# Two blocks in fp32 on one core: the moving operands of FFN matmuls read in two halves by turns

## The reference

```python
def swiglu(h, w_gate, w_up, w_down):
    return (jax.nn.silu(h @ w_gate) * (h @ w_up)) @ w_down
# h: 256 x 1024, w_gate and w_up: 1024 x 2816, w_down: 2816 x 1024
# first stack, twice per layer:  x = x + 0.5 * swiglu(rmsnorm(x, g), w_gate, w_up, w_down)
# second stack, once per layer:
gu = x @ w_gate_up[l]
hidden = jax.nn.silu(gu[..., :D_FF_2]) * gu[..., D_FF_2:]
x = _layer_norm(DEEPNORM_ALPHA * x + hidden @ w_down[l], ln2_g[l], ln2_b[l])
```

## Time and profile before

| | us |
|---|---|
| median of 2 runs | 2010.06 (2009.33 to 2010.79) |
| span of the profiled execution | 2008.8 |
| PE busy in the span | 1995.9 (99%) |
| PE weight loads busy | 1934.1 (96%) |
| DVE busy | 1238.7 (62%) |
| ACT busy | 997.1 (50%) |
| DMA engines, mean busy share of the slices | about one half |

### The profile page before, as it was taken

How to read it: one execution, slowest core, us unless ns; L and a number is a source line. 1 busy time by engine, 2 the same in 40 slices (tenths; PEclk the granted TensorE clock), 3 DMA queues, 4 the chain that set the end, 5 groups by cost and what they waited for, 6 DMA issues and landing times.

```text
span 2008.8 us, 37237 instructions
## 1 busy us (share of the span) xinstructions
PE 1995.9 (99%) x15798; PEld 1934.1 (96%) x15798; DVE 1238.7 (62%) x1214; ACT 997.1 (50%) x997; POOL 55.2 (3%) x49
## 2 busy tenths in 40 slices
PE   9999999999999999999999999999999999999998
PEld 8999999999999999899999999999998999999997
DVE  7556665755675576766556664585447574576445
ACT  6545655544454457654444575444444573644442
POOL 3000000100010000010000000000000000000000
PEclk9999999999999999999999999999999999999999
DMA  8555453455555554345554453555554544564552
GB/s 306 189 188 188 169 171 145 167 189 188 188 195 187 186 186 147 126 153 213 188 188 169 179 189 128 213 206 189 188 186 158 191 167 149 210 224 162 187 187 100
DMA packets 52913, 363.29 MB, mean 181 GB/s; under 512 B 5960, under 2 KB 7120, under 8 KB 9808
## 3 DMA queue, kind: packets, MB, share of 16 engines
q1 hardware_dynamic: 51200, 352.99, 48.9%
q0 software_dynamic: 1616, 8.86, 1.2%
HBM read 360.76 MB, written 1.06 MB: 180 GB/s over the span
## 4 chain that ended last, share of the span: by engine, by line
PE 95%; DVE 3%; ACT 1%; DMA 1%; issue 0%; DVEq 0%; SPq 0%; ACTq 0%
PE ps L277 21%; PE ps L279 21%; PE ps L278 21%; PE ps L322 4%; PE ps L323 4%; PE ps L324 4%; PE ps L560 3%; PE ps L561 3%; PE ps L559 3%; PE ps L543 1%; PE ps L537 1%; PE ps L538 1%; PE ps L1864 1%; PE ps L843 1%; DMA raw<-in_slots 1%; PE ps L311 1%
## 5 line engine op out<-in xcount | busy, mean ns | idle before, releaser
L247 DVE TENSOR_TENSOR wlo<-raw,whi 128x2048 fp32r<-128x2048 f32 x322 | 742.9, 2309 | 421.0 <-ACT whi L242 420.2
L277 PE MATMUL ps<-in_hi,whi 128*128 128x256 f32 x3236 | 909.6, 281 | 1.1 <-DVE in_lo L652 0.9
L278 PE MATMUL ps<-in_lo,whi 128*128 128x256 f32 x3236 | 903.4, 279 | 0.0
L279 PE MATMUL ps<-in_hi,wlo 128*128 128x256 f32 x3236 | 902.4, 279 | 0.0
L242 ACT ACTIVATE whi<-raw 128x2048 fp32r<-128x2048 f32 x322 | 614.5, 1910 | 196.6 <-PE ps L279 173.8
L277 PEld LDWEIGHTS ps<-in_hi,whi 128*128 128x128 f32 x3236 | 608.2, 188 | 4.8 <-DVE wlo L263 1.4
L278 PEld LDWEIGHTS ps<-in_lo,whi 128*128 128x128 f32 x3236 | 608.3, 188 | 2.3 <-issue 0.7
L279 PEld LDWEIGHTS ps<-in_hi,wlo 128*128 128x128 f32 x3236 | 608.3, 188 | 0.0
L322 PE MATMUL ps<-whi,in_hi 128*128 128x256 f32 x640 | 181.4, 283 | 0.0
L323 PE MATMUL ps<-wlo,in_hi 128*128 128x256 f32 x640 | 179.8, 281 | 0.0
L324 PE MATMUL ps<-whi,in_lo 128*128 128x256 f32 x640 | 179.8, 281 | 0.0
(11 more groups left out here) (318 smaller groups left out, 2188.2 us busy)
## 6 DMA issues: line engine op xcount, KB each, us to landing
raw<-in_slots SPq DMA_DIRECT2D x330, 1024.0 KB, 4.8
ws<-in_lngb POOLq DMA_DIRECT2D x4, 1024.0 KB, 6.0
raw<-in_slots SPq DMA_DIRECT2D x12, 256.0 KB, 5.6
ws<-in_mem_t POOLq DMA_DIRECT2D x2, 1024.0 KB, 10.2
consts<-in_consts SPq DMA_DIRECT2D x1, 1536.0 KB, 9.6
consts<-in_consts POOLq DMA_DIRECT2D x1, 1472.0 KB, 8.1
x<-in_x_t SPq DMA_DIRECT2D x4, 256.0 KB, 5.1
ws<-m_rows POOLq DMA_DIRECT2D x2, 512.0 KB, 5.5
```

The costliest lines, as they stand in the source:

```text
L247: dve.tensor_tensor(wlo[:, j], raw[:, j], whi[:, j].bitcast(F32), ALU.subtract).then_inc(lo_ready, 1)
L277: pe.matmul(out, whi[:, j, o:o + n], hi, start=start, stop=False, skip_group_check=True)
L278: pe.matmul(out, whi[:, j, o:o + n], lo, start=False, stop=False, skip_group_check=True)
L279: return pe.matmul(out, wlo[:, j, o:o + n], hi, start=False, stop=stop, skip_group_check=True)
```

## The change

The change touches only the access patterns of some matmuls. The new helper `halves_by_turns(v, run)` takes a view of n columns, cuts it into two halves of n/2 columns, and walks them by turns: `run` columns of the first half, `run` columns of the second, the next `run` of the first, and so on. It is applied to the moving operand and to the output alike, so each product lands where it did, and only the order in which the columns pass through PE is another. For 256 columns the two halves are 512 bytes apart in SBUF and in PSUM, for 512 columns 1024 bytes. With `run` None the view stays as it was. The stationary operands, the number of instructions, their order on every engine, the waits and the DMAs stay as they were.

```diff
+        def halves_by_turns(v, run):
+
+            return v if run is None else v.rearrange("p (s a b) -> p a s b", s=2, b=run)
+
-        def pe_pair(pe, out, j, at=range(DT)):
+        def pe_pair(pe, out, j, at=range(DT), run=None):
 
             for m in range(2):
                 for k in range(DT):
-                    last = pe_weight(pe, out[:, m * T:(m + 1) * T], j, k * 256 + m * P, in_hi[:, at[k]], in_lo[:, at[k]],
+                    last = pe_weight(pe, halves_by_turns(out[:, m * T:(m + 1) * T], run), j, k * 256 + m * P,
+                                     halves_by_turns(in_hi[:, at[k]], run), halves_by_turns(in_lo[:, at[k]], run),
                                      k == 0, k == DT - 1)
             return last
+
+        GATE_RUN = (None, 4, 8, 2, 64, None)
+        DOWN_RUN = (None, None, None, 8, 4, 2)
...
-                pe_pair(pe, out, (c + s) % RING).then_inc(slot_used, 1)
+                pe_pair(pe, out, (c + s) % RING, run=GATE_RUN[f]).then_inc(slot_used, 1)
...
-        def pe_down_part(pe, j, hi, lo, t, h, first=False):
+        def pe_down_part(pe, j, hi, lo, t, h, run, first=False):
 
-            o, a = ps[:, 2 * t + h, :], slice(t * P, (t + 1) * P)
+            o, a = halves_by_turns(ps[:, 2 * t + h, :], run), slice(t * P, (t + 1) * P)
             for kk in range(2):
                 w = slice(kk * D + h * 512, kk * D + h * 512 + 512)
-                pe.matmul(o, hi[:, kk, a], whi[:, j, w], start=(first and kk == 0), stop=False, skip_group_check=True)
-                pe.matmul(o, hi[:, kk, a], wlo[:, j, w], start=False, stop=False, skip_group_check=True)
-                last = pe.matmul(o, lo[:, kk, a], whi[:, j, w], start=False, stop=False, skip_group_check=True)
+                pe.matmul(o, hi[:, kk, a], halves_by_turns(whi[:, j, w], run), start=(first and kk == 0), stop=False, skip_group_check=True)
+                pe.matmul(o, hi[:, kk, a], halves_by_turns(wlo[:, j, w], run), start=False, stop=False, skip_group_check=True)
+                last = pe.matmul(o, lo[:, kk, a], halves_by_turns(whi[:, j, w], run), start=False, stop=False, skip_group_check=True)
             return last
```

More of the change, by code:

```diff
@@ L570, in gate @@
                 pe.wait_ge(ffn_silu, fb + i)
-                pe_pair(pe, gate_ps, (c + s) % RING).then_inc(slot_used, 1)
+                pe_pair(pe, gate_ps, (c + s) % RING, run=GATE_RUN[f]).then_inc(slot_used, 1)
             def up(i, s, i3):
@@ L575, in up @@
                 pe.wait_ge(ffn_mul, fb + i)
-                pe_pair(pe, up_ps, (c + s) % RING).then_inc(slot_used, 1)
+                pe_pair(pe, up_ps, (c + s) % RING, run=GATE_RUN[f]).then_inc(slot_used, 1)
             def down(i, s, i3, first=False):
@@ L582, in down @@
                     for h in range(2):
-                        last = pe_down_part(pe, (c + s) % RING, h_hi, h_lo, t, h, first)
+                        last = pe_down_part(pe, (c + s) % RING, h_hi, h_lo, t, h, DOWN_RUN[f], first)
                 last.then_inc(slot_used, 1)
@@ L621, in pe_ffn_tok @@
             for h in range(2):
-                pe_down_part(pe, s9 % RING, h_hi, h_lo, 0, h)
+                pe_down_part(pe, s9 % RING, h_hi, h_lo, 0, h, DOWN_RUN[f])
             pe.wait_ge(lo_ready, s10 + 1)
@@ L625, in pe_ffn_tok @@
             for h in range(2):
-                pe_down_part(pe, s10 % RING, last_hi, last_lo, 0, h).then_inc(down_half, 1)
+                pe_down_part(pe, s10 % RING, last_hi, last_lo, 0, h, DOWN_RUN[f]).then_inc(down_half, 1)
             for h in range(2):
-                last = pe_down_part(pe, s9 % RING, h_hi, h_lo, 1, h)
+                last = pe_down_part(pe, s9 % RING, h_hi, h_lo, 1, h, DOWN_RUN[f])
             last.then_inc(slot_used, 1)
-            pe_down_part(pe, s10 % RING, last_hi, last_lo, 1, 0).then_inc(down_half, 1)
+            pe_down_part(pe, s10 % RING, last_hi, last_lo, 1, 0, DOWN_RUN[f]).then_inc(down_half, 1)
             if m_out is not None:
                 pe_turn_y(pe, m_out, 0)
-            pe_down_part(pe, s10 % RING, last_hi, last_lo, 1, 1).then_inc(slot_used, 1)
+            pe_down_part(pe, s10 % RING, last_hi, last_lo, 1, 1, DOWN_RUN[f]).then_inc(slot_used, 1)
         def wait_down(dve, f, t, h):
```

## The result

The changed kernel takes 2109.15 us (median of 2 runs, 2108.17 to 2110.14) against 2010.06 us: ratio 1.049, 95% interval 1.0473 to 1.0507. It is slower by 5%; I had forecast no change; the time lies inside the range of 1990 to 2165 us, which was as wide as it was for a rival's sake (runs of 2 at half pace).

What follows compares the result with a forecast made beforehand. PE's own stream was taken to bound the kernel. The terms, 3840 x 0 + 792 x 0 = 0, left the 2008.8 us span, whose runs' median lies 1.3 us higher: 2010 us, range 1990 to 2165 for 8 in 10.

Steps and rivals of the forecast that it cites:

- What bounds the kernel: Whole kernel: PE's own stream is the time, busy 1995.9 of 2008.8 us, so each nanosecond on a matmul counts.
- Counts: Matmuls the change touches: 3840 gate and up of 256 columns in four FFNs, 792 down of 512 columns.
- No other engine hides or adds anything: FFN 4 round of 16.80 us: DVE busy 8.26, ACT 6.76, DMA 53%; PE could be 8% faster without running into them.
- The price per column: Changed gate, up and down matmuls, 634 us: pace stays 0.456 ns per column, 0 us added; chance of this forecast 0.60.
- The stall that I had measured myself: Plain fp32r stream: as if standing still 1.25 ns after every 32 columns, 116.7 ns for 256 where the clock allows 106.7.
- Half pace for runs of 2: Gate and up of FFN 3, down of FFN 5: plain fp32's pace, 95 + 52 us, 2158 us in all; chance 0.18.
- the case that I held likeliest: Whole kernel: no change in pace, or a few ns in one run; 2010 us, own range 1998 to 2040.
- A price per jump: All changed matmuls: every jump costs the 1.25 ns stall, dearer for shorter runs; 372 us more, 2382 us; chance 0.14.
- The stall goes away: Changed matmuls: alternating two places gives a bank time, removing the stall; 1962 us in full; chance 0.08, full or part.
- The bound of 48 us: Changed matmuls: the most the order could save by removing the stall, 25 + 9 + 14 us.
- The ratio of 256 to 512 columns: FFN 3 slots: 116.7 and 233.3 ns, exactly as their columns, so nothing is a cost per instruction or weight load.
- The rules of the Trainium skill: Changed matmuls: line rule gives 2010 us, non-contiguous rule slows all 634 us; issue-gap rule estimates 109.2 and 215.8 ns.

## Why the prediction was right and wrong

- *What bounds the kernel*: right. PE's stream is the time, and each ns of a matmul appeared in full; the table of slots gives the span's growth without a rest.
- *Counts*: 3840 and 792 matmuls, right. *No other engine hides or adds anything*: right.
- *The price per column, "I take 0"*: this step failed. I argued that the pace cares neither for the length nor for the place of the operand, and took it for a pace of the datapath that needs only two neighbours side by side. Plain streams of two lengths can't show that: both use whole lines one behind the other. In place of 0 the runs showed 8.9, 6.6, 49.9 and 0.5 ns per gate or up matmul for runs of 4, 8, 2 and 64, and 9.2, 20 and about 101 ns per down matmul for runs of 8, 4 and 2. The price is in reading the moving operand (2109.95 us with it alone turned, 2014.33 with the output alone), and it hangs on two things: whether a run fills aligned lines of 16 bytes (126.7 against 171 ns for runs of 4 moved by 8 bytes), and the step between the runs (113.4 to 139.0 ns for the same whole lines). How the reader works behind this stays open. The stall that I had measured myself was a sign that the stream had little to spare.
- *Half pace for runs of 2*: the right mechanism (more bytes come than the run uses, and they are thrown away), and the right place, between 2 and 4. The size was off: 95 and 52 us were forecast, 48 and 27 measured, since from two halves such runs take 166.6 ns; the 216 were borrowed from plain fp32, which has another reason to be slow. That runs of 2 take 226.6 ns from four parts, near the 216, is no merit of the working. And it is luck that the time lies in the range: the range came from this rival at twice its size, not from the case that I held likeliest (1998 to 2040).
- *A price per jump*: the order 64, 8, 4, 2 came out as this rival had it (117.2, 123.3, 126.7, 166.6 ns), but at 0.2 ns and not 1.25 ns a jump, and the shift by 8 bytes made the same jumps dear.
- *The stall goes away*: partly true, at a step that the change does not use. The bound of 48 us for the changed matmuls was too high: at 114.9 and 226.7 ns they would save an estimated 13 us (2880 x 1.8, 960 x 2.9 and 792 x 6.6 ns), and the 34 us found come from nearly all fp32r matmuls of the kernel. The ratio of 256 to 512 columns had told me that nothing is a cost per instruction or weight load; the floor of 111.4 ns was hidden, since it lies just under the 116.7 ns of the plain order.
- *The rules of the Trainium skill*: "Advanced Engine Details and Errata", section Memory Cachelines, asks for two hits on a 16-byte line. The runs agree with a line of that size, but two hits are not enough for fp32r: 166.6 to 233 ns against 116.7. Its other half, that a non-contiguous pattern slows matmuls, is said there of PSUM, and is not borne out here: the output turned alone left every slot at its pace. The estimate of 216 ns by "TensorE: Matmul & The Clock Gate", section Back-to-back issue gap, of the Trainium skill holds for bf16 with 512 columns (216 measured) and not for fp32r (233.3).

## What to carry to other kernels

Ask first whether each run of a moving operand fills whole, aligned lines of 16 bytes. In fp32r, runs that did cost from 3 ns less to 22 ns more per 256 columns, and runs that used half a line 50 to 116 ns more. A bf16 stream has more to spare: its runs of 8 bytes cost 5%, its runs of 4 bytes 26%. Then measure the step between the runs, since no count of lines or jumps here gives the price. And when a stream is slower than the clock allows, try the order of its columns: an order at no cost in instructions gave 1.7% here.

## What the runs showed of the hardware that I had not expected

- Reading in runs of 16 bytes at a step of 64 bytes is faster than reading in the order of addresses: 226.7 against 233.3 ns for 512 columns, 114.9 against 116.7 for 256. At a step of 256 bytes the same whole lines take 139.0 ns per 256 columns.
- fp32r instructions with 128 moving columns take 111.4 ns each, nearly what 256 columns do (116.7). The weight load of 128 columns is the likely floor; it was not measured apart.
- The output order was free: with the outputs alone in runs of 2, 4, 8 and 64 from two halves, slots kept 116.7 and 233.3 ns.
- Where tiles lie matters by some ns even in plain order: in the kernel with `in_hi` and `in_lo` moved, plain slots took 120.0 ns against 116.7, also those whose moving operand was another tile. The cause is open.
- The 1 ns more of FFN 1 (117.7 ns) also came and went in other kernels and, in FFN 4 of the changed one, from round to round (116.7 and 117.8). Its cause is open.
